# Attention of a two-layer encoder in double steps: scores, values and output splits of two query tiles at a time

## The chip, the cores and the metric

One core of a Trainium2 chip runs the whole kernel. The metric is the device time of one execution in microseconds (us), smaller is better. Engines: TensorE (PE; its weight loads are PEld), VectorE (DVE), ScalarE (ACT), GpSimd (POOL), SyncE (SP, which only issues transfers here).

## The reference

Two layers over x of 512 tokens x 1024 features. Layer 0 mixes tokens by attention, layer 1 by gated linear attention; each is followed by a gated ConvFFN. The change touches the attention alone:

```
def swa_sink_attention(h, w_qkv, sinks, rel_bias, w_o):   # query chunk c (64 tokens) reads key chunks c-1 and c
    qkv = h @ w_qkv                                       # 16 query heads of 64, 4 key/value heads
    ...
    scores = einsum('bnqhgd,bnjhd->bhgnqj', q, k_band) * (A_HEAD_DIM ** -0.5) + bias   # band of 128 keys
    scores = where(valid, scores, NEG)                    # the first chunk has no chunk before it
    m = maximum(scores.max(axis=-1), sink)
    p = exp(scores - m[..., None])
    p = p / (p.sum(axis=-1) + exp(sink - m))[..., None]
    out = einsum('bhgnqj,bnjhd->bnqhgd', p, v_band)
    return out.reshape(B, S, A_HEADS * A_HEAD_DIM) @ w_o
```

## The kernel before

Activations lie feature by token, in 128-row tiles of 512 tokens. Every projection is done in split precision: a weight tile is cast to a rounded high part (ScalarE, `hi_unit`, L950), the low part is raw minus high (VectorE, `lo_unit`, L1389), and TensorE forms high x high, high x low and low x high (`product`, L485). A unit is one 128-column block of outputs: 8 blocks of the contraction, 24 products of 512 columns. Units are numbered: 4 to 11 are the queries (`A_Q` on), 12 to 19 the output projection (`A_O` on). The queries of KV head g need units 4 + 2g and 5 + 2g. A unit u waits for `lo_ready` u + 1 and for its bank; four weight slots are loaded by SyncE as earlier units end.

The attention stage is a hand-written list on each engine, joined by semaphores, with a loop over k = 0 to 15. Step k is KV head g = k // 4 and token tile p = k % 4 (two chunks j, two head halves). TensorE, for k: half a projection unit (or, from k = 12, half of an output unit's contraction), `scores(k)` (L667), `turn_probs(k - 2)` (four transposes, L675), `values(k - 3)` (L685). VectorE, for k: `softmax_max(k)` (adds scale and bias, L1767, row maximum, L1770, and three small ones), at odd k `queries` (L1750), `o_lo(k - 3)` (L1788), `lo_unit`, `softmax_divide(k - 1)` (L1780 to L1782). ScalarE: `probs_copy(k - 2)` (L1206), `o_hi(k - 3)` (L1218), `softmax_exp(k)` (four exponentials with row sums, L1198, and one small), `hi_unit`. In step k = 2 VectorE makes the low part of unit 8, which TensorE starts in step 4, and so on in twos; each engine's list is executed strictly in order.

KT holds the keys of each KV head twice, once with rows 64 to 127 zero and once with rows 0 to 63 zero, so that a contraction over all 128 rows of QT (two heads) picks one head. `values` writes its two head halves to rows 0 to 63 and 64 to 127 of bank B7, from 64 columns of V each. After the loop the output units get the rest of their contraction; the last two blocks of each wait for the last `o_lo`. Before the loop GpSimd fills the bias table (L2028, L2030), and clears KT (L2021, L2022) before SyncE's loads of constants.

Of the kernel before, what the change touches and what calls it, by code (L numbers as in the profile page):

```python
# [31 lines left out]
P = 128  # L32
# [63 lines left out]
def trunk(nc, xT, gains, w_qkv, sinks, rel_bias, w_o, w_bin, w_ga, w_gate, b_norm, w_bo, w_up, conv_w, conv_b,  # L96
          w_down0, w_down1, onehot, ident, causal, causal_pair, out, bias_rows):
    with ExitStack() as ctx:
# [100 lines left out]
        KT = place("KT", [P, KV, 2, T])  # L199
# [6 lines left out]
        BIAS = place("BIAS", [P, KV, 4, P])  # L206
# [265 lines left out]
        def _(pe):  # L472
# [178 lines left out]
            def scores(k):  # L651

                g, p = divmod(k, 4)
                if k == 0:
                    pe.wait_ge(std_ready, 1)
                    pe.wait_ge(v_copied, 4)
                    pe.wait_ge(k_dup, 64)
                if k >= 2:
                    pe.wait_ge(s_ready, k - 1)
                if p == 0:  # L660
                    pe.wait_ge(unit_evac, A_Q + 2 * g + 2)
                for j in range(2):
                    for half in range(2):
                        q, keys = QT[:, g % 2, 2 * p + j], KT[:, g, half]
                        c = (2 * j + half) * P
                        first = max(2 * p - 1 + j, 0) * CHUNK
                        last = mm(PS[:, B4 + k % 2, c:c + P], q, keys[:, first:first + P], start=True, stop=True)  # L667
                last.then_inc(scores_done, 1)
# [9 lines left out]
            def values(k):  # L678
                g, p = divmod(k, 4)
                pe.wait_ge(pt_ready, k + 1)  # L680
                if k >= 1:
                    pe.wait_ge(ol_ready, k)
                for j in range(2):
                    for half in range(2):
                        last = mm(PS[64 * half:64 * half + 64, B7, j * P:(j + 1) * P],  # L685
                                  V[:, 1 - j if p else 0, p, g * HD:(g + 1) * HD], PT[:, k % 2, 2 * j + half],
                                  start=True, stop=True)
# [5 lines left out]
            for k in range(16):  # L693
                g, p = divmod(k, 4)


                if g < 3:
                    u = A_Q + 2 + k // 2
                    if k % 2 == 0:
                        pe.wait_ge(lo_ready, u + 1)  # L700
                        pe.wait_ge(unit_evac, u - 3)
                    last = out_part(u, range(4 * (k % 2), 4 * (k % 2) + 4), XH, XL, k % 2 == 0, k % 2 == 1)
                    if k % 2 == 1:
                        last.then_inc(unit_done, 1)
                else:
                    u = A_O + p
                    pe.wait_ge(lo_ready, u + 1)
                    pe.wait_ge(unit_evac, u - 3)
                    pe.wait_ge(ol_ready, 8)
                    out_part(u, range(0, 4), OH, OL, True, False)  # L710
                scores(k)
                if k >= 2:
                    turn_probs(k - 2)
                if k >= 3:
                    values(k - 3)
            pe.wait_ge(ol_ready, 12)
            out_part(A_O, range(4, 6), OH, OL, False, False)
            turn_probs(14)
            values(13)
            out_part(A_O + 1, range(4, 6), OH, OL, False, False)  # L720
            turn_probs(15)
            values(14)
            out_part(A_O + 2, range(4, 6), OH, OL, False, False)
            values(15)
            out_part(A_O + 3, range(4, 6), OH, OL, False, False)
            pe.wait_ge(ol_ready, 16)
# [218 lines left out]
        def _(act):  # L945
# [227 lines left out]
            for hh in range(2):  # L1173
                for half in range(2):
                    rows = slice(64 * hh, 64 * hh + 64)
                    act.dma_start(BIAS[rows, :, 2 + half],
# [4 lines left out]
            for g in range(KV):  # L1181
# [3 lines left out]
                act.dma_start(KT[there, g, 1 - g % 2], KT[here, g, g % 2]).then_inc(k_dup, 16)  # L1185
# [16 lines left out]
            def probs_copy(k):  # L1202
                act.wait_ge(pt_done, k + 1)
                if k >= 2:
                    act.wait_ge(pv_done, k - 1)
                nc.scalar.copy(PT[:, k % 2], PS[:, B6].rearrange("p (i c) -> p i c", i=4)).then_inc(pt_ready, 1)  # L1206

            def o_view(k):

                return PS[:, B7, 0:2 * P].rearrange("p (j a q) -> p a j q", j=2, a=2)  # L1210

            def o_tiles(t, k):
                g, p = divmod(k, 4)
                return t[:, 2 * g:2 * g + 2, p * P:(p + 1) * P].rearrange("p a (j q) -> p a j q", j=2)

            def o_hi(k):
                act.wait_ge(pv_done, k + 1)
# [960 lines left out]
```

## Time and profile before

| | us |
|---|---|
| median of 3 runs | 1079.18 (1078.86 to 1079.74) |
| the profiled execution, its own time | 1078.77 |
| its span | 1076.9 |
| TensorE busy | 1067.1 (99%) |
| VectorE busy | 752.5 (70%) |
| ScalarE busy | 494.1 (46%) |
| GpSimd busy | 113.8 (11%) |

The profile shows one execution. Busy times are sums over an engine's instructions; the chain that ended last is followed back from the last instruction, at each step to what released it. Matmuls are pipelined: a product's row in the timeline is longer than the distance to the next one's start, and the distance is what it costs. The attention loop lies between about 43 and 128 us.

### The profile page before, as it was taken

Reading aid. Unit: us, or ns where it says so; the run is one execution under the profiler, and the core shown is the slowest. Engines: PE = TensorE matmul, PEld = TensorE weight load, DVE = VectorE, ACT = ScalarE, POOL = GpSimd, SP = SyncE. Lnnn points to the kernel's source line nnn. Section 1 sums busy time; section 2 is a strip of 40 time slices with the busy share of each in tenths; the row PEclk is TensorE's granted clock in tenths of the full one; section 3 lists DMA queues with packets and bytes.
Section 4 is the critical chain, followed back from the end, with each engine's and each line's share of the span. In section 5 each row is a group of like instructions: output and inputs, shape, how many; then the busy total and the mean of one; then the engine's idle time right before and its main releaser. Section 6 shows DMA issues by size and latency. Waiting matters only on the chain.

```text
span 1076.9 us, 15711 instructions
## 1 busy us (share of the span) xinstructions
PE 1067.1 (99%) x5930; PEld 917.5 (85%) x5930; DVE 752.5 (70%) x1097; ACT 494.1 (46%) x769; POOL 113.8 (11%) x108
## 2 busy tenths in 40 slices
PE   9999999999999999999999999999999999999997
PEld 7888788888899888899888888888888899888897
DVE  6588667677876667789644556867676876667786
ACT  7366554434433343455652345454444433334443
POOL 2100030000100000123020321130000100000122
PEclk9999999999999999999999999999999999999999
DMA  7611032226653225552222211222225652225552
GB/s 228 154 59 60 22 115 98 97 97 185 162 134 107 98 97 170 129 140 99 97 74 85 97 40 59 73 105 97 97 97 185 162 147 96 97 97 170 135 141 92
DMA packets 43804, 121.12 MB, mean 112 GB/s; under 512 B 5250, under 2 KB 10530, under 8 KB 43748
## 3 DMA queue, kind: packets, MB, share of 16 engines
q1 hardware_dynamic: 36020, 106.55, 29.7%
q0 software_dynamic: 4608, 11.54, 6.6%
q10 hardware_dynamic: 3120, 2.28, 1.1%
q8 instruction: 37, 0.61, 0.2%
q14 instruction: 19, 0.16, 0.0%
HBM read 116.93 MB, written 2.88 MB: 111 GB/s over the span
## 4 chain that ended last, share of the span: by engine, by line
PE 93%; DVE 4%; DMA 1%; ACT 1%; issue 1%; SPq 0%; POOL 0%; DVEq 0%; POOLq 0%
PE PS L485 69%; PE PS L545 18%; PE PS L667 1%; PE PS L685 1%; DMA DRAW_W<-w_down 1%; PE PS L675 1%; DVE STD L1896 1%; DMA X<-xT 1%; PE PS L836 1%; DVE WL L1389 1%; PE PS L746 0%; PE PS L849 0%; PE PS L773 0%; DVE EU L1900 0%; PE PS L786 0%
## 5 line engine op out<-in xcount | busy, mean ns | idle before, releaser
L485 PE MATMUL PS<-XH,WH 128*128 128x512 f32 x992 | 391.4, 395 | 1.4 <-DVE XL L1406 1.4
L485 PE MATMUL PS<-XH,WL 128*128 128x512 f32 x992 | 386.4, 390 | 0.0
L485 PE MATMUL PS<-XL,WH 128*128 128x512 f32 x992 | 386.1, 389 | 0.0
L485 PEld LDWEIGHTS PS<-XH,WH 128*128 128x128 f32 x992 | 186.2, 188 | 42.5 <-issue 4.6
L485 PEld LDWEIGHTS PS<-XH,WL 128*128 128x128 f32 x992 | 186.2, 188 | 39.1
L485 PEld LDWEIGHTS PS<-XL,WH 128*128 128x128 f32 x992 | 186.3, 188 | 38.8 <-issue 1.0
L950 ACT CAST WH<-WRAW 128x1024 fp32r<-128x1024 f32 x134 | 139.5, 1045 | 158.3 <-DMA WRAW<-w_up 106.9
L1389 DVE TENSOR_TENSOR WL<-WRAW,WH 128x1024 fp32r<-128x1024 f32 x134 | 165.1, 1233 | 16.4 <-ACT WH L950 15.7
L1427 DVE TENSOR_TENSOR GS<-PS,R 128x512 f32<-128x512 f32 x44 | 30.4, 692 | 118.5 <-PE PS L485 118.5
L545 PE MATMUL PS<-AH,DH_Z 128*128 128x256 f32 x352 | 97.7, 278 | 0.2
L545 PE MATMUL PS<-AH,DL_Z 128*128 128x256 f32 x352 | 97.2, 276 | 0.0
L545 PE MATMUL PS<-AL,DH_Z 128*128 128x256 f32 x352 | 97.2, 276 | 0.0
L993 ACT ACTIVATE CV<-GS,CONVB,CONVW 128x512 f32<-128x512 f32 x44 | 36.1, 820 | 91.8 <-DVE GS L1427 91.8
L545 PE MATMUL PS<-AH,DH_W 128*128 128x256 f32 x264 | 73.5, 279 | 0.2
L545 PE MATMUL PS<-AH,DL_W 128*128 128x256 f32 x264 | 72.9, 276 | 0.0
L545 PE MATMUL PS<-AL,DH_W 128*128 128x256 f32 x264 | 72.9, 276 | 0.0
L1522 DVE TENSOR_TENSOR X<-X,PS 128x256 f32<-128x256 f32 x112 | 46.1, 416 | 34.0 <-PE PS L545 33.5
L545 PEld LDWEIGHTS PS<-AH,DH_Z 128*128 128x128 f32 x352 | 66.1, 188 | 2.0 <-PE PS L485 1.9
L545 PEld LDWEIGHTS PS<-AL,DH_Z 128*128 128x128 f32 x352 | 66.1, 188 | 0.0
L545 PEld LDWEIGHTS PS<-AH,DL_Z 128*128 128x128 f32 x352 | 66.1, 188 | 0.0
L1027 ACT CAST DH_W<-DRAW_W 128x768 fp32r<-128x768 f32 (+1 forms) x48 | 37.0, 780 | 53.7 <-DMA DRAW_W<-w_down 53.6
L545 PEld LDWEIGHTS PS<-AH,DH_W 128*128 128x128 f32 x264 | 49.6, 188 | 0.6 <-DVE X L1522 0.6
(236 smaller groups left out, 1508.1 us busy)
## 6 DMA issues: line engine op xcount, KB each, us to landing
WRAW<-w_up SPq DMA_DIRECT2D x88, 512.0 KB, 3.3
WRAW<-w_bin SPq DMA_DIRECT2D x24, 512.0 KB, 3.2
DRAW_W<-w_down SPq DMA_DIRECT2D x24, 384.0 KB, 3.8
DRAW_W<-w_down SPq DMA_DIRECT2D x24, 320.0 KB, 3.0
WSUM_Z<-w_down SPq DMA_DIRECT2D x12, 384.0 KB, 4.7
WSUM_Z<-w_down POOLq DMA_DIRECT2D x12, 384.0 KB, 6.3
WRAW<-w_qkv SPq DMA_DIRECT2D x8, 512.0 KB, 3.4
WSUM_Z<-w_down SPq DMA_DIRECT2D x12, 320.0 KB, 3.8
```

What stands on the lines that cost most here:

```text
L485: last = mm(PS[:, bank], w[:, c:c + P], x[:, kb], start=start and n == 0 and w is wh and x is hi, stop=stop and n == len(kbs) - 1 and w is wl)
L545: last = mm(PS[:, bank, 0:TH], w[:, c], act_part[:, kb, x], start=start and kb == 0 and w is DH[name] and act_part is AH, stop=kb == PAIRS ...
L667: last = mm(PS[:, B4 + k % 2, c:c + P], q, keys[:, first:first + P], start=True, stop=True)
L675: last = nc.tensor.transpose(PS[:, B6, i * P:(i + 1) * P], PB[:, k % 2, i], IDENT[:])
L685: last = mm(PS[64 * half:64 * half + 64, B7, j * P:(j + 1) * P], V[:, 1 - j if p else 0, p, g * HD:(g + 1) * HD], PT[:, k % 2, 2 * j + hal ...
L836: mm(PS[:, B6 + p // 2, (p % 2) * HV:(p % 2 + 1) * HV], KUT[:, p], VV[:, p, h * HV:(h + 1) * HV], start=True, stop=True).then_inc(u_done, 1)
L950: nc.scalar.copy(WH[s][:], WRAW[s][:]).then_inc(hi_ready, 1)
L993: A(CV[:, par], GS[:, par, 2:T + 2], ACT.Identity, bias=CONVB[:, layer, tile], scale=CONVW[:, layer, tile, 2]).then_inc(c0_ready, 1)
L1027: nc.scalar.copy(DH[name][:, c], raw[:, c]).then_inc(down_hi[name], 1)
L1389: tt(WL[s][:], WRAW[s][:], WH[s][:].bitcast(F32), ALU.subtract).then_inc(lo_ready, 1)
L1427: tt(GS[:, par, 2:T + 2], PS[:, 2 * par], R[:], ALU.mult).then_inc(unit_evac, 2)
L1522: tt(x, x, PS[:, SETS[n % 2][bank], 0:TH], op).then_inc(x_taken, 1)
```

## The change

Pairs of token tiles are worked at a time in parts of the lists. `scores(pair)` makes the scores of two tiles at once: KT holds each key head once in both row halves, each product contracts over 64 rows only, head half 0 into bank B4 and half 1 into B5, 16 of TensorE's products per pair in place of 2 x 8. `values(pair)` and the output split (`o_hi`, `o_lo`) also take both tiles at once, 512 columns in place of 256. The transposes stay per tile, each behind one half projection unit (`between(pair, half)`). The softmax stays per tile; its four parts are ordered by head, then chunk. The bias table gets an own copy for the first tile, filled in three GpSimd copies. All four lists are written out anew. VectorE's list of a pair has both `softmax_max` first; `queries` and `lo_unit` stand between the two `softmax_divide`. In pair 1 that is `lo_unit(8)`, and unit 8 is the one of TensorE's pair 2.

```diff
--- before.py
+++ after.py
@@ -196,14 +196,14 @@
         place_at[0] = region
-        KT = place("KT", [P, KV, 2, T])
+        KT = place("KT", [P, KV, T])
         VT = place("VT", [P, 2, T])
...
         PT = place("PT", [P, 2, 4, P])
-        BIAS = place("BIAS", [P, KV, 4, P])
+        BIAS = place("BIAS", [P, 2, KV, 4, P])
         TB = place("TB", [P, REL])
...
@@ -648,23 +648,24 @@
...
-            def scores(k):
-
-                g, p = divmod(k, 4)
+            def scores(pair):
+
+                g, p = pair // 2, 2 * (pair % 2)
+                k = 2 * pair
                 if k == 0:
...
                     pe.wait_ge(k_dup, 64)
-                if k >= 2:
-                    pe.wait_ge(s_ready, k - 1)
+                if k >= 1:
+                    pe.wait_ge(s_ready, k)
                 if p == 0:
                     pe.wait_ge(unit_evac, A_Q + 2 * g + 2)
-                for j in range(2):
+                for j in range(4):
+                    first = max(2 * p - 1 + j, 0) * CHUNK
                     for half in range(2):
-                        q, keys = QT[:, g % 2, 2 * p + j], KT[:, g, half]
-                        c = (2 * j + half) * P
-                        first = max(2 * p - 1 + j, 0) * CHUNK
-                        last = mm(PS[:, B4 + k % 2, c:c + P], q, keys[:, first:first + P], start=True, stop=True)
+                        rows = slice(64 * half, 64 * half + 64)
+                        q, keys = QT[rows, g % 2, 2 * p + j], KT[rows, g]
+                        last = mm(PS[:, B4 + half, j * P:(j + 1) * P], q, keys[:, first:first + P], start=True, stop=True)
                 last.then_inc(scores_done, 1)
             def turn_probs(k):
@@ -675,55 +676,62 @@
...
-            def values(k):
-                g, p = divmod(k, 4)
-                pe.wait_ge(pt_ready, k + 1)
-                if k >= 1:
-                    pe.wait_ge(ol_ready, k)
-                for j in range(2):
-                    for half in range(2):
-                        last = mm(PS[64 * half:64 * half + 64, B7, j * P:(j + 1) * P],
-                                  V[:, 1 - j if p else 0, p, g * HD:(g + 1) * HD], PT[:, k % 2, 2 * j + half],
-                                  start=True, stop=True)
+            def values(pair):
+                g = pair // 2
+                pe.wait_ge(pt_ready, 2 * pair + 2)
+                if pair >= 1:
+                    pe.wait_ge(ol_ready, pair)
+                for k in range(2):
+                    p = 2 * (pair % 2) + k
+                    for j in range(2):
+                        c = (2 * k + j) * P
+                        for half in range(2):
+                            last = mm(PS[64 * half:64 * half + 64, B7, c:c + P],
+                                      V[:, 1 - j if p else 0, p, g * HD:(g + 1) * HD], PT[:, k, 2 * half + j],
+                                      start=True, stop=True)
                 last.then_inc(pv_done, 1)
             def out_part(u, kbs, hi, lo, start, stop):
...
-            for k in range(16):
-                g, p = divmod(k, 4)
-
-
-                if g < 3:
-                    u = A_Q + 2 + k // 2
-                    if k % 2 == 0:
+            def between(pair, half):
+
+                if pair < 6:
+                    u = A_Q + 2 + pair
+                    if half == 0:
                         pe.wait_ge(lo_ready, u + 1)
                         pe.wait_ge(unit_evac, u - 3)
-                    last = out_part(u, range(4 * (k % 2), 4 * (k % 2) + 4), XH, XL, k % 2 == 0, k % 2 == 1)
-                    if k % 2 == 1:
+                    last = out_part(u, range(4 * half, 4 * half + 4), XH, XL, half == 0, half == 1)
+                    if half == 1:
                         last.then_inc(unit_done, 1)
                 else:
-                    u = A_O + p
+                    u = A_O + 2 * (pair - 6) + half
                     pe.wait_ge(lo_ready, u + 1)
                     pe.wait_ge(unit_evac, u - 3)
-                    pe.wait_ge(ol_ready, 8)
+                    pe.wait_ge(ol_ready, 4)
                     out_part(u, range(0, 4), OH, OL, True, False)
-                scores(k)
-                if k >= 2:
-                    turn_probs(k - 2)
-                if k >= 3:
-                    values(k - 3)
-            pe.wait_ge(ol_ready, 12)
+
+            for pair in range(8):
+                between(pair, 0)
+                scores(pair)
+                if pair >= 2:
+                    values(pair - 2)
+                if pair >= 1:
+                    turn_probs(2 * pair - 2)
+                between(pair, 1)
+                if pair >= 1:
+                    turn_probs(2 * pair - 1)
+            pe.wait_ge(ol_ready, 6)
             out_part(A_O, range(4, 6), OH, OL, False, False)
+            values(6)
             turn_probs(14)
-            values(13)
             out_part(A_O + 1, range(4, 6), OH, OL, False, False)
             turn_probs(15)
-            values(14)
-            out_part(A_O + 2, range(4, 6), OH, OL, False, False)
-            values(15)
+            out_part(A_O + 2, range(4, 5), OH, OL, False, False)
+            values(7)
+            out_part(A_O + 2, range(5, 6), OH, OL, False, False)
             out_part(A_O + 3, range(4, 6), OH, OL, False, False)
-            pe.wait_ge(ol_ready, 16)
+            pe.wait_ge(ol_ready, 8)
             for u in range(A_O, A_O + 4):
...
@@ -1173,7 +1181,7 @@
...
                     rows = slice(64 * hh, 64 * hh + 64)
-                    act.dma_start(BIAS[rows, :, 2 + half],
+                    act.dma_start(BIAS[rows, 1, :, 2 * half + 1],
                                   bass.AP(tensor=bias_rows.tensor,
...
@@ -1182,7 +1190,7 @@
...
                 here, there = slice(64 * (g % 2), 64 * (g % 2) + 64), slice(64 - 64 * (g % 2), 128 - 64 * (g % 2))
-                act.dma_start(KT[there, g, 1 - g % 2], KT[here, g, g % 2]).then_inc(k_dup, 16)
+                act.dma_start(KT[there, g], KT[here, g]).then_inc(k_dup, 16)
             hi_unit(6)
...
@@ -1202,38 +1210,30 @@
             def probs_copy(k):
...
                 if k >= 2:
-                    act.wait_ge(pv_done, k - 1)
+                    act.wait_ge(pv_done, k // 2)
                 nc.scalar.copy(PT[:, k % 2], PS[:, B6].rearrange("p (i c) -> p i c", i=4)).then_inc(pt_ready, 1)
-            def o_view(k):
-
-                return PS[:, B7, 0:2 * P].rearrange("p (j a q) -> p a j q", j=2, a=2)
-
-            def o_tiles(t, k):
-                g, p = divmod(k, 4)
-                return t[:, 2 * g:2 * g + 2, p * P:(p + 1) * P].rearrange("p a (j q) -> p a j q", j=2)
-
-            def o_hi(k):
-                act.wait_ge(pv_done, k + 1)
-                nc.scalar.copy(o_tiles(OH, k), o_view(k)).then_inc(oh_ready, 1)
-
-            for k in range(16):
-                g, p = divmod(k, 4)
-                if k >= 2:
-                    probs_copy(k - 2)
-                if k >= 3:
-                    o_hi(k - 3)
-                softmax_exp(k)
-                if k % 2 == 0 and k <= 8:
-                    hi_unit(8 + k // 2)
-                elif 9 <= k <= 12 and k != 10:
-                    hi_unit(k + 3 if k > 9 else 13)
-                elif k == 14:
-                    hi_unit(A_O + 4)
-            for k in range(14, 16):
-                probs_copy(k)
-                o_hi(k - 1)
-            o_hi(15)
+            def o_hi(pair):
+                g, tokens = pair // 2, slice(pair % 2 * TH, pair % 2 * TH + TH)
+                act.wait_ge(pv_done, pair + 1)
+                nc.scalar.copy(OH[:, 2 * g:2 * g + 2, tokens].rearrange("p a (x q) -> p a x q", x=4),
+                               PS[:, B7].rearrange("p (x a q) -> p a x q", x=4, a=2)).then_inc(oh_ready, 1)
+
+            for pair in range(8):
+                if pair >= 2:
+                    o_hi(pair - 2)
+                if pair >= 1:
+                    probs_copy(2 * pair - 2)
+                softmax_exp(2 * pair)
+                for u in ((8,), (9,), (10,), (11,), (12, 13), (14,), (15,), (16,))[pair]:
+                    hi_unit(u)
+                if pair >= 1:
+                    probs_copy(2 * pair - 1)
+                softmax_exp(2 * pair + 1)
+            o_hi(6)
+            probs_copy(14)
+            probs_copy(15)
+            o_hi(7)
             for m in range(6):
...
@@ -1736,7 +1736,7 @@
...
                     rows = slice(64 * half, 64 * half + 64)
-                    last = tt(KT[rows, 2 * t + half, half], PS[rows, t], R[rows], ALU.mult)
+                    last = tt(KT[rows, 2 * t + half], PS[rows, t], R[rows], ALU.mult)
                 last.then_inc(unit_evac, 1)
...
@@ -1758,18 +1758,16 @@
             def softmax_max(k):
...
                 if k == 0:
-                    dve.wait_ge(bias_ready, 2)
-                dve.wait_ge(scores_done, k + 1)
+                    dve.wait_ge(bias_ready, 4)
+                dve.wait_ge(scores_done, k // 2 + 1)
                 b = k % 2
-                items = lambda t: t.rearrange("p (j x) -> p j x", j=2)
-                bias = BIAS[:, g].rearrange("p i c -> p (i c)")
-                bias = items(bias) if p == 0 else bias[:, 2 * P:].unsqueeze(1).to_broadcast([P, 2, 2 * P])
-                stt(items(SB[:, b].rearrange("p i c -> p (i c)")), items(PS[:, B4 + b]), A_SCALE, bias,
+                by_head = lambda t: t.rearrange("p (h j) c -> p h (j c)", h=2)
+                stt(by_head(SB[:, b]), PS[:, B4:B4 + 2, 2 * b * P:2 * (b + 1) * P], A_SCALE, by_head(BIAS[:, min(p, 1), g]),
                     ALU.mult, ALU.add).then_inc(s_ready, 1)
...
                 link(nc.vector.tensor_reduce(MX[:, b], SB[:, b], AX.X, ALU.max))
-                sink = SINK[:, g:g + 1, :].to_broadcast([P, 2, 2])
-                two = lambda t: t[:, b].rearrange("p (j h) -> p j h", j=2)
+                sink = SINK[:, g].unsqueeze(2).to_broadcast([P, 2, 2])
+                two = lambda t: t[:, b].rearrange("p (h j) -> p h j", h=2)
                 link(tt(two(MX), two(MX), sink, ALU.max))
...
@@ -1781,32 +1779,27 @@
...
-            def o_lo(k):
-                g, p = divmod(k, 4)
-                dve.wait_ge(oh_ready, k + 1)
-                view = lambda t: t[:, 2 * g:2 * g + 2, p * P:(p + 1) * P].rearrange("p a (j q) -> p a j q", j=2)
-                tt(view(OL), PS[:, B7, 0:2 * P].rearrange("p (j a q) -> p a j q", j=2, a=2), view(OH).bitcast(F32),
+            def o_lo(pair):
+                g, tokens = pair // 2, slice(pair % 2 * TH, pair % 2 * TH + TH)
+                dve.wait_ge(oh_ready, pair + 1)
+                view = lambda t: t[:, 2 * g:2 * g + 2, tokens].rearrange("p a (x q) -> p a x q", x=4)
+                tt(view(OL), PS[:, B7].rearrange("p (x a q) -> p a x q", x=4, a=2), view(OH).bitcast(F32),
                    ALU.subtract).then_inc(ol_ready, 1)
-            for k in range(16):
-                g, p = divmod(k, 4)
-                softmax_max(k)
-
-                if g < 3 and k % 2 == 1:
-                    queries(A_Q + 2 + k // 2)
-                if k >= 3:
-                    o_lo(k - 3)
-                if k % 2 == 0 and 2 <= k <= 10:
-                    lo_unit(7 + k // 2)
-                elif 11 <= k <= 13:
-                    lo_unit(k + 2)
-                if k >= 1:
-                    softmax_divide(k - 1)
-            softmax_divide(15)
-            o_lo(13)
+            for pair in range(8):
+                softmax_max(2 * pair)
+                softmax_max(2 * pair + 1)
+                if pair >= 2:
+                    o_lo(pair - 2)
+                softmax_divide(2 * pair)
+                if pair < 6:
+                    queries(A_Q + 2 + pair)
+                for u in ((), (8,), (9,), (10,), (11,), (12, 13), (14, 15), ())[pair]:
+                    lo_unit(u)
+                softmax_divide(2 * pair + 1)
+            o_lo(6)
             lo_unit(A_O + 4)
-            o_lo(14)
-            o_lo(15)
+            o_lo(7)
             for m in range(6):
...
@@ -2017,18 +2010,19 @@
...
             pool.wait_ge(eps_set, 1)
-            link(nc.gpsimd.memset(WG[:], 0.0))
-            link(nc.gpsimd.memset(KT[64:P, :, 0], 0.0))
-            nc.gpsimd.memset(KT[0:64, :, 1], 0.0).then_inc(small_set, 1)
+            nc.gpsimd.memset(WG[:], 0.0).then_inc(small_set, 1)
             pool.wait_ge(small_set, 1)
...
             pool.wait_ge(bias_in, 16 * 4)
-            nc.gpsimd.memset(BIAS[:, :, 0:2, 64:P], NEG).then_inc(bias_ready, 1)
+            nc.gpsimd.memset(BIAS[:, 0, :, ::2, 64:P], NEG).then_inc(bias_ready, 1)
             pool.wait_ge(bias_ready, 1)
-            nc.gpsimd.tensor_copy(BIAS[:, :, 0:2, 0:64], BIAS[:, :, 2:4, 64:P]).then_inc(bias_ready, 1)
-            pool.wait_ge(bias_ready, 2)
+            loaded = BIAS[:, 1, :, 1::2]
+            for n, (to, src) in enumerate(((BIAS[:, 0, :, ::2, 0:64], BIAS[:, 1, :, 1::2, 64:P]),
+                                           (BIAS[:, 0, :, 1::2], loaded), (BIAS[:, 1, :, ::2], loaded))):
+                nc.gpsimd.tensor_copy(to, src).then_inc(bias_ready, 1)
+                pool.wait_ge(bias_ready, n + 2)
...
             pool.wait_ge(consts, 16 * CONSTS)

```

## Rows read from the trace of the kernel before

**Rows 1.** Page, part 4: the chain that ended last, its shares by engine.

```profile
PE 93%; DVE 4%; DMA 1%; ACT 1%; issue 1%; SPq 0%; POOL 0%; DVEq 0%; POOLq 0%
```

**Rows 2.** Windows: busy us (and instructions) of PE, PEld, DVE, ACT, POOL; granted clock.

```profile
46.00:128.40 82.40, 81.52 (x527) 66.69 (x526) 62.90 (x159) 51.74 (x185) 0.00 (x0) 1.00 0.14 47
```

**Rows 3.** Chain in order of time (start us, us, what) for one step.

```profile
74.47 2.94 PE PS L485 x12
77.42 0.89 PE PS L667 x8
...
79.33 2.94 PE PS L485 x12
```

**Rows 4.** Timeline of TensorE (start us, us, line, output, inputs), one step and the end.

```profile
83.00 0.60 PE L675 MATMUL PS<-IDENT,PB 128*128 128x128 f32 x4
...
83.53 0.33 PE L685 MATMUL PS<-PT,V 128*64 128x128 f32 x2
...
83.53 0.55 PE L685 MATMUL PS<-PT,V 128*64 128x128 f32 x6
...
84.46 0.39 PE L485 MATMUL PS<-XL,WH 128*128 128x512 f32 x1
...
128.36 0.40 PE L485 MATMUL PS<-OH,WH 128*128 128x512 f32 x1
```

**Rows 5.** Timeline of VectorE over one step of the loop.

```profile
80.14 0.69 DVE L1750 TENSOR_TENSOR QT<-PS,R 128x512 f32<-128x512 f32 x1
80.74 0.42 DVE L1788 TENSOR_TENSOR OL<-PS,OH 128x256 fp32r<-128x256 f32 x1
...
83.20 0.69 DVE L1767 SCALAR_TENSOR_TENSOR SB<-PS,BIAS 128x512 f32<-128x512 f32 x1 [1.04 <-PE PS L667]
...
85.00 0.41 DVE L1788 TENSOR_TENSOR OL<-PS,OH 128x256 fp32r<-128x256 f32 x1
85.33 1.21 DVE L1389 TENSOR_TENSOR WL<-WRAW,WH 128x1024 fp32r<-128x1024 f32 x1
86.47 0.15 DVE L1780 TENSOR_TENSOR RD<-SUM,ES 128x4 f32<-128x4 f32 x1
...
86.86 0.69 DVE L1782 TENSOR_TENSOR PB<-PB,RD 128x512 f32<-128x512 f32 x1
```

**Rows 6.** Timeline of ScalarE over one step of the loop.

```profile
78.78 0.59 ACT L1206 COPY PT<-PS 128x512 f32<-128x512 f32 x1 [0.70 <-PE PS L675]
79.38 0.37 ACT L1218 CAST OH<-PS 128x256 fp32r<-128x256 f32 x1
80.27 0.40 ACT L1198 ACTIVATE PB<-SB,NM 128x128 f32<-128x128 f32 x1 [0.52 <-DVE NM L1775]
...
81.83 0.19 ACT L1200 ACTIVATE ES<-SM 128x4 f32<-128x4 f32 x1
```

**Rows 7.** Timeline of the other queues before the loop, and its first scores.

```profile
5.20 1.92 SPq L413 DMA_DIRECT2D WRAW<-w_qkv  x3
...
39.94 0.61 POOL L2030 COPY BIAS<-BIAS 128x512 f32<-128x512 f32 x1
...
46.18 1.05 PE L667 MATMUL PS<-KT,QT 128*128 128x128 f32 x8
...
47.35 0.69 DVE L1767 SCALAR_TENSOR_TENSOR SB<-PS,BIAS 128x512 f32<-128x512 f32 x1 [3.00 <-PE PS L667]
```

**Rows 8.** Windows (last columns: granted clock, DMA share, GB/s) and timeline of TensorE, first and last products.

```profile
1.00 2.93 PE L622 MATMUL PS<-STD 128*128 128x128 f32 x12 [1.00 <-POOL STD L2016]
...
3.72 1.47 PE L622 MATMUL PS<-STD 128*128 128x128 f32 x11
...
1070.80 0.72 PE L922 MATMUL PS<-STD,ONESR 128*128 128x128 f32 x5
...
1075.70:1076.80 1.10, 0.00 (x0) 0.50 0.28 90
```

**Rows 9.** Waits of TensorE in this stretch: us in total, times, longest.

```profile
PE PS L675 <- DVE PB L1782: 0.9, 2, 0.7
```

## The prediction

> **What bounds the kernel now.** I read the page first: TensorE holds 93% of the chain that ended last [rows 1]. So a change pays only if it takes work off TensorE without making TensorE wait. Next the stage table for the attention stretch, 46 to 128.4 us: TensorE 81.5 of 82.4 us, VectorE 62.9, ScalarE 51.7 [rows 2]. VectorE has a quarter of the stretch free and ScalarE more than a third, but only because each has work of neighbouring steps to interleave. Then the chain: it never leaves TensorE over most of the loop, and one step from a half projection unit (2.94) over scores (0.89), transposes and values to the next half unit is 79.33 - 74.47 = 4.86, so two steps take 9.72 [rows 3]. The stretch ends at 128.36, where the last two blocks of the output units begin [rows 4]. Last the timelines of the three engines over one step [rows 4 to 6]. Times below are from the span's start. A duration that is followed by more work counts from start to start.
>
> **TensorE's part.** A plain product of 512 columns takes 0.228 (the 2.94 of 12, less 0.21 that belongs to the values before them, below), so a half unit takes 2.74. Scores: 8 products (each f32 product is two in the trace) of 0.11 make 0.89. Transposes: 4 x 0.11 = 0.44. Values already work in two column halves: two products start together and each further two add 0.11 ((0.55 - 0.33)/2), so 8 take 0.44 [rows 4]. Their step is dearer than that. The transposes began at 83.00 and were through at 83.44, and the next unit's second product starts at 84.46, which without any cost of changing shape would be 83.44 + 0.44 + 0.23 = 84.11. So one burst in halves costs 0.35 on top: 0.14 going in (0.09 before the first pair, 0.05 in it), 0.21 coming out. I cost a values burst at 0.80 now.
> After the change scores run as two 64-row halves into two banks, for which the trace has no row. The nearest are those values: 16 products in 8 pairs, 0.88 + 0.35 = 1.22 where two bursts of 0.89 took 1.78. From below, with no cost of changing, it is 0.88; from above, with no overlap, 1.78 + 0.35 = 2.12. I take 1.22, since both are halves of the array used in turn. Values of a pair: 0.87 + 0.35 = 1.22 for 1.60. The work per pair on TensorE falls from 9.72 to 2 x 2.74 + 1.22 + 1.22 + 2 x 0.44 = 8.8. Over 8 pairs that is 4.5 + 3.0 = 7.5 us less.
> The Trainium skill (TensorEngine Tiling (Array Packing), Key Properties) says that switching the tiling mode drains the engine, and the same page (Theoretical Speedup) gives up to 2x for a contraction of 64. The 0.35 above agrees with the drain. By the 2x alone scores would take 0.88 and the total below would be 2.1 us less; by the drain it stands as I have it.
>
> **Where the weights' low parts go.** This decides it. Before, `lo_unit(8)` runs in step 2 and its unit starts in step 4, `lo_unit(9)` in step 4 for step 6: two steps of slack. After, VectorE's list puts `lo_unit(8)` into pair 1, behind both `softmax_max`, `softmax_divide(2)` and `queries`, and TensorE's pair 2 *begins* with unit 8 and waits for it; the same with 9, 10, 11, 12 and 14 in pairs 2 to 6. Behind that wait stand the half unit and the next scores, on which VectorE's next pair waits. So the two engines take turns, and the loop is their sum.
> VectorE's leg, from the end of the last score product: start 0.20 later (83.20 against 83.00); two `softmax_max` of 1.80 (83.20 to 85.00), 3.60; `o_lo` of a pair, 512 columns from PSUM, 0.60 (as the QT row, 80.14 to 80.74); divide 0.40 + 0.60 = 1.00; queries 0.60; low part 1.21; and 0.15 until TensorE has its first product through [rows 4, 5]. Sum 7.36.
> TensorE's leg: half unit 2.74, scores to the end of their last product 0.14 + 0.88 = 1.02. The loop is 11.1 us.
> ScalarE has a side leg into it: scores' coming out 0.21, values 1.22 and 0.14, `o_hi` of 512 columns 0.60 and the copy of the transposes 0.60 (78.78 to 79.38), four exponentials and the small one 1.75 (80.27 to 82.02) [rows 6]: the divide can start at 4.55, where VectorE comes to it at 4.40. If scores and values, which stand side by side, share one change of shape, these 0.15 go. I take half: **11.2 us per pair, against 9.72**. TensorE works 8.8 of them and stands idle 2.4.
> The wait of the units for `unit_evac` and of scores for `s_ready` are met long before: nothing.
>
> **The sum.** Scores of pair 0 start at 46.18 [rows 7]. 1.22 and two half units: scores of pair 1 at 52.9, done 53.9. VectorE: 47.4 + 3.6 = 51.0, divide(0) behind its exponentials to 52.1, the second ones (behind ScalarE's cast of unit 8) end at 53.8, divide(1) at 54.9; then 3.6, 0.1 of waiting, divide, queries and low part give 61.4. TensorE was through at 57.8, idles 3.8, and starts scores of pair 2 at 64.3. Four more turns of 11.2: 109.0. The last has no queries, 10.6: scores of pair 7 at 119.6. Behind them TensorE has, without a wait over 0.1: 1.22 + 1.22 + 0.44 + 2.74 + 0.44, then 6 products 1.37, values 1.22, 0.44, 1.37, 0.44, 0.68, values 1.3, 0.68, 1.37 = 14.9: 134.5. Before it was 128.36 [rows 4]. The difference is **+6.2 us**.
> Against the profiled execution that is 1076.9 + 6.2 = 1083.1 of span and 1078.8 + 6.2 = 1085.0 of time; that run lay 0.4 below the median of the three, so the median should be 1079.2 + 6.2 = **1085.4**. After the stretch TensorE's queue is the same and it is the bound, so nothing gives the loss back.
>
> **Edits that cost nothing.** The bias table is completed by two more GpSimd copies of 1024 columns; one of 512 took 0.61, so they add 2.5 at most, and the table is ready at 43.1 where the first use is at 47.35: cover 4.2, and every us beyond it would be lost whole [rows 7]. The constants for GA behind them (0.96 and less each) are used some 350 us later. Two memsets of KT go from GpSimd; SyncE, which waits for them before it issues the constants, is itself busy issuing weights until 7.1 [rows 7], so that earlier memsets start nothing earlier. The copies of K between halves move the same bytes on the same queue. The mask and the sink only change order.
>
> **The rivals.** *No overlap of row halves.* 0.9 more in each of six turns, in pair 0 to 1 and in little else: 6.6 more, 1092.0. For it: no row shows 64-row halves. Against: column halves overlap fully [rows 4].
> *The clock falls in the gaps.* At the end the granted clock is 0.50, that is 1.2 GHz, from 1075.7, and the last product had ended at 1071.4: 4.3 us without work [rows 8]. At the start products come every 0.23 ((2.93 - 0.4)/11) from 1.0 until 3.7, and from 3.72 every 0.11 ((1.47 - 0.35)/10): 2.7 us at the low level, so a fall costs some 1.4. The first gap is 3.8, the others 2.4, all shorter than 4.3. One fall gives 1086.8, six 1093.6. The Trainium skill (TensorE: Matmul & The Clock Gate, on throughput drops) warns that idle gaps between bursts send the engine back to half rate; the rows agree that idle time does it, and have no gap of 2.4 or 3.8.
> *TensorE stays the bound.* If the low part is ready when TensorE comes to it, the kernel gains the 7.5 and the 0.9 of waits for PB [rows 9]: 1070.8, faster. It needs a turn of 8.8, VectorE's 7.36 down to 5.0; the gain ends where the turn is 10.2. Against: all its terms are measured on the same shapes, and the order is in the queues. A turn between 10 and 10.4 is the case of no difference.
>
> **How the numbers follow.** Forecast 0.80; no overlap 0.07; clock 0.04; TensorE bound 0.05; in between, no difference 0.04. So slower 0.91, same 0.04, faster 0.05, with 0.2% as about what a measurement of this kernel tells from no change. The forecast's own range is 1082 (scores at 0.88, shapes changed for nothing) to 1088. The range takes in the upper bound of the row halves, 1092.5, and leaves out the gain.
>
> **What would show it.** The chain should run through WL, QT, PB and SB in the stretch; TensorE should wait some 3.8 + 4 x 2.4 + 1.8 = 15 us for WL, six times; the first output block should start near 134.5; two score products should start within 0.01 of each other. I am wrong if TensorE does not wait for WL, or if scores of successive pairs stand 8.8 or over 12 us apart.

## The result and the profile after

The changed kernel takes 1091.1 us (median of 5, 1089.66 to 1091.48) against 1079.56 for the one before (median of 5): ratio 1.0107, 95% interval 1.0096 to 1.0118. Slower by 11.5 us, where 6.2 were forecast. The profiled execution took 1089.66, with a span of 1087.9: 11.0 more than the span before. The median lies 1.4 above it. That is about the price of one more fall of the clock (below), but that execution left no trace, so this is a guess.

The page of the changed kernel: TensorE's busy tenths and the clock it was granted, each in 40 slices of 27 us, and the shares of the chain.

```profile
PE   9978899999999999999999999999999999999997
...
PEclk9989999999999999999999999999999999999999
...
PE 89%; DVE 7%; ACT 2%; DMA 1%; issue 1%; SPq 0%; POOL 0%; DVEq 0%; POOLq 0%
```

TensorE holds 89% of the chain where it held 93% [rows 1]. VectorE's share is 7% for 4%, ScalarE's 2% for 1%, and in the third to fifth slices of TensorE's row (54 to 136 us, the attention) it is no longer busy all the time; the clock's third slice shows a dip that was not there before. The timeline of TensorE, of the lines that matter: every start of a pair's scores (L668), and every product that had to wait (in brackets: how long, and for whom). L485 is a product of a unit, WL the low part of its weights.

```profile
53.21 1.16 PE L668 MATMUL PS<-KT,QT 64*128 64x128 f32 x16
...
61.61 0.74 PE L485 MATMUL PS<-XH,WH 128*128 128x512 f32 x1 [3.47 <-DVE WL L1389]
...
66.16 1.16 PE L668 MATMUL PS<-KT,QT 64*128 64x128 f32 x16
...
74.43 0.50 PE L485 MATMUL PS<-XH,WH 128*128 128x512 f32 x1 [2.28 <-DVE WL L1389]
...
78.96 1.16 PE L668 MATMUL PS<-KT,QT 64*128 64x128 f32 x16
...
87.23 0.50 PE L485 MATMUL PS<-XH,WH 128*128 128x512 f32 x1 [2.28 <-DVE WL L1389]
...
90.20 1.16 PE L668 MATMUL PS<-KT,QT 64*128 64x128 f32 x16
...
98.47 0.50 PE L485 MATMUL PS<-XH,WH 128*128 128x512 f32 x1 [2.29 <-DVE WL L1389]
...
103.00 1.16 PE L668 MATMUL PS<-KT,QT 64*128 64x128 f32 x16
...
111.27 0.50 PE L485 MATMUL PS<-OH,WH 128*128 128x512 f32 x1 [2.29 <-DVE WL L1389]
...
114.21 1.16 PE L668 MATMUL PS<-KT,QT 64*128 64x128 f32 x16
...
121.89 0.50 PE L485 MATMUL PS<-OH,WH 128*128 128x512 f32 x1 [1.70 <-DVE WL L1389]
```

Six waits for WL, of 3.5, four times 2.3, and 1.7 us, 14.3 together, where the kernel before had 0.9 for PB [rows 9] and the forecast some 15. The scores of pairs 1 to 7 start 12.95, 12.80, 11.24, 12.80, 11.21 and 10.6 us apart (a turn; the last pair's start at 124.83), where two steps took 9.72 [rows 3]. The forecast had 11.4, 11.2 and 10.6. So three turns are as worked out, and three are 1.55 to 1.6 too long. What sets a turn is in the chain, here of the fourth, from the scores to the next unit's products:

```profile
90.27 1.12 PE PS L668 x16
...
95.99 0.69 DVE PB L1780
96.69 0.60 DVE QT L1750
97.28 1.14 DVE WL L1389
...
98.47 4.60 PE PS L485 x12
```

The chain goes over to VectorE behind the scores and comes back only with WL, 7.1 us later: the engines take turns. Why that turn is 12.80 and not 11.2 is in the windows (columns: busy PE, PEld, DVE, ACT, POOL; granted clock, DMA share, GB/s).

```profile
61.70:65.10 3.40, 3.40 (x8) 2.67 (x9) 1.03 (x3) 0.05 (x1) 0.00 (x0) 0.50 0.00 0
65.10:74.40 9.30, 7.04 (x57) 5.46 (x55) 6.73 (x16) 5.97 (x22) 0.00 (x0) 1.00 0.17 55
75.40:78.80 3.40, 3.40 (x9) 2.34 (x8) 0.14 (x1) 0.00 (x0) 0.00 (x0) 0.50 0.00 0
99.30:102.60 3.30, 3.30 (x9) 2.61 (x8) 1.02 (x3) 0.00 (x0) 0.00 (x0) 0.50 0.00 0
```

In three stretches of about 3.4 us (one row for each that shows the half clock) TensorE was granted half the clock (1.2 GHz), each beginning within 1 us after one of the gaps, in the half unit that everybody waits for. After the other gaps of 2.3 us it was not. A turn with such a stretch is 12.80, one without 11.24.

One mark serves all comparisons below, the product of L506, the first work behind the output units: everything that the attention loses or gains is in by then. From the chain of the kernel before, and of the changed one:

```profile
161.18 0.23 PE PS L506
```

```profile
172.32 0.23 PE PS L506
```

11.1 us lost by there, and 11.0 over the span. Nothing is given back or lost later.

What TensorE itself takes. Timeline of one pair of the changed kernel, scores, values, and the transposes after them:

```profile
90.20 1.16 PE L668 MATMUL PS<-KT,QT 64*128 64x128 f32 x16
91.29 1.09 PE L689 MATMUL PS<-PT,V 128*64 128x128 f32 x16
92.32 0.66 PE L676 MATMUL PS<-IDENT,PB 128*128 128x128 f32 x4
```

Scores take 1.09 and values 1.03, 2.12 together for 32 products that stream in 16 pairs of 0.11, 1.76. Before, a pair of steps took 2 x 0.89 and 2 x 0.80 for them. The halves of 64 rows do overlap. The 2.12 leaves out what the change of shape costs before the first and behind the last of these products. Counted as the prediction counted its 0.35, from the product before to the second product behind, the two bursts cost 0.50 over their streaming (a burst: all scores, or all values, of a step or pair).

### The profile page after: what moved, and what is told of

Read it like the earlier page. It is cut to its first block, busy times and chain, and to the rows that moved or that the text cites. A ratio compares the mean times of both kernels' runs of the same rounds, so it can differ in the third digit from the quotient of the medians.

```text
span 1087.9 us, 15687 instructions
## 1 busy us (share of the span) xinstructions
PE 1065.7 (98%) x5930; PEld 914.5 (84%) x5930; DVE 751.3 (69%) x1089; ACT 491.3 (45%) x761; POOL 113.4 (10%) x108
## 4 chain that ended last, share of the span: by engine, by line
PE 89%; DVE 7%; ACT 2%; DMA 1%; issue 1%; SPq 0%; POOL 0%; DVEq 0%; POOLq 0%
PE PS L485 65%; PE PS L545 19%; DVE WL L1389 1%; DVE MX L1768 1%; DVE SB L1765 1%; PE PS L668 1%; DMA X<-xT 1%; DVE STD L1889 1%; PE PS L844 1%; DVE PB L1780 0%; DVE SS L1710 0%; ACT PB L1206 0%; PE PS L754 0%; DMA DRAW_W<-w_down 0%; PE PS L857 0%
## 5 line engine op out<-in xcount | busy, mean ns | idle before, releaser
L485 PE MATMUL PS<-XH,WH 128*128 128x512 f32 x992 | 393.4, 397 | 10.3 <-DVE WL L1389 10.3
L485 PE MATMUL PS<-XL,WH 128*128 128x512 f32 x992 | 388.1, 391 | 0.0
L485 PE MATMUL PS<-XH,WL 128*128 128x512 f32 x992 | 388.1, 391 | 0.0
L485 PEld LDWEIGHTS PS<-XH,WH 128*128 128x128 f32 x992 | 187.1, 189 | 51.1 <-DVE WL L1389 11.3
L485 PEld LDWEIGHTS PS<-XH,WL 128*128 128x128 f32 x992 | 187.5, 189 | 39.8
L485 PEld LDWEIGHTS PS<-XL,WH 128*128 128x128 f32 x992 | 187.5, 189 | 39.2 <-issue 1.0
L545 PE MATMUL PS<-AH,DH_Z 128*128 128x256 f32 x352 | 97.7, 278 | 0.2
L545 PE MATMUL PS<-AH,DL_Z 128*128 128x256 f32 x352 | 97.3, 276 | 0.0
L545 PE MATMUL PS<-AL,DH_Z 128*128 128x256 f32 x352 | 97.3, 276 | 0.0
L545 PE MATMUL PS<-AH,DH_W 128*128 128x256 f32 x264 | 73.5, 279 | 0.1
L545 PE MATMUL PS<-AH,DL_W 128*128 128x256 f32 x264 | 73.0, 276 | 0.0
L545 PE MATMUL PS<-AL,DH_W 128*128 128x256 f32 x264 | 73.0, 276 | 0.0
L545 PEld LDWEIGHTS PS<-AH,DH_Z 128*128 128x128 f32 x352 | 66.1, 188 | 1.9 <-PE PS L485 1.9
L545 PEld LDWEIGHTS PS<-AL,DH_Z 128*128 128x128 f32 x352 | 66.2, 188 | 0.0
L545 PEld LDWEIGHTS PS<-AH,DL_Z 128*128 128x128 f32 x352 | 66.1, 188 | 0.0
L545 PEld LDWEIGHTS PS<-AH,DH_W 128*128 128x128 f32 x264 | 49.6, 188 | 0.3 <-DVE X L1522 0.3
```

The lines of the kernel that those rows point to most:

```text
L485: last = mm(PS[:, bank], w[:, c:c + P], x[:, kb], start=start and n == 0 and w is wh and x is hi, stop=stop and n == len(kbs) - 1 and w is wl)
L545: last = mm(PS[:, bank, 0:TH], w[:, c], act_part[:, kb, x], start=start and kb == 0 and w is DH[name] and act_part is AH, stop=kb == PAIRS ...
```

## The experiments

Theory A is that of the prediction, with the clock added: the low parts of the weights are made in the pair before their use, behind everything else of VectorE, so that TensorE and VectorE take turns; and the gaps that this opens make the clock fall. Theory B, in e1, is that the double step itself is the loss; the others are in each expectation. Each median is set against the runs of the kernel before on the same chip: 1079.57 for the first four, 1078.90 for the last three.

**e1, low parts one pair earlier.**

```diff
-                for u in ((), (8,), (9,), (10,), (11,), (12, 13), (14, 15), ())[pair]:
+                for u in ((8,), (9,), (10,), (11,), (12, 13), (14,), (15,), ())[pair]:
                     lo_unit(u)
```

> The changed kernel with VectorE's low parts one pair earlier (units 8, 9, 10, 11, 12 and 13, 14, 15 in pairs 0 to 6 in place of 1 to 6), all else the same. Theory A (TensorE and VectorE take turns because the low part is made in the pair before its use, behind everything else, and the clock falls in the gaps that this opens): the waits of TensorE for WL go, scores of successive pairs stand 8.7 us apart, no fall of the clock in the stretch; 1071, between 1069 and 1073. Theory B (the double step itself costs: long bursts, two shapes of the array, both softmax_max in a row): the waits move to another place, and the time stays over 1079.

Measured 1070.24 (1069.63 to 1071.26), ratio 0.9917, interval 0.9900 to 0.9935. TensorE's timeline:

```profile
60.66 1.16 PE L668 MATMUL PS<-KT,QT 64*128 64x128 f32 x16
...
69.31 1.16 PE L668 MATMUL PS<-KT,QT 64*128 64x128 f32 x16
```

Its window (busy PE; clock, DMA share, GB/s), and the mark:

```profile
44.00:120.00 76.00, 75.95 (x540) 1.00 0.17 57
```

```profile
151.75 0.23 PE PS L506
```

Pairs are 8.65 us apart (one of them, from pair 5 to 6, 8.95), no product of TensorE waits in the stretch, and the granted clock is 1.00 over it. The mark lies 9.4 before that of the kernel before, 20.6 before that of the changed kernel. The place of the low parts in VectorE's list is the whole loss and 9 us more. Theory B falls. This is the fastest of all versions here.

**e2, the gaps filled.** The products go into the bank that the unit is about to start, and are overwritten.

```diff
                     if half == 0:
-                        pe.wait_ge(lo_ready, u + 1)
                         pe.wait_ge(unit_evac, u - 3)
+                        for _ in range({2: 14, 3: 9, 4: 9, 5: 9}.get(pair, 0)):
+                            mm(PS[:, u % 4, 0:P], ONES, ONES, start=True, stop=True)
+                        pe.wait_ge(lo_ready, u + 1)
```

and the same for pairs 6 and 7 (9 and 6 products) in the other branch.

> The changed kernel with TensorE kept at work while it waits for the low part: 14 f32 products of 128 columns into the still empty bank before unit 8, 9 each before units 9 to 12, 6 before unit 14, each 0.22 us at full clock. Nothing else changes. Theory A: the clock is 1.00 over the whole stretch, all turns are 11.2 us (the last 10.6), and what the falls cost goes: 1.6 each for three or four falls, 1086 (1085 to 1087). Theory B (the falls have another cause than the gaps, say the products of half the array's rows): the clock falls as before and the time stays at 1091. Theory C (the filling delays the real work by more than it saves): over 1091.

Measured 1087.00 (1086.25 to 1088.26), ratio 1.0069, interval 1.0050 to 1.0087.

```profile
70.22 2.17 PE L704 MATMUL PS<-ONESR 128*128 128x128 f32 x18
72.69 0.50 PE L485 MATMUL PS<-XH,WH 128*128 128x512 f32 x1 [0.29 <-DVE WL L1393]
...
75.67 1.16 PE L668 MATMUL PS<-KT,QT 64*128 64x128 f32 x16
...
86.89 1.16 PE L668 MATMUL PS<-KT,QT 64*128 64x128 f32 x16
```

```profile
44.00:136.00 92.00, 90.16 (x653) 74.26 (x652) 62.44 (x152) 48.72 (x177) 1.77 (x5) 1.00 0.14 47
```

```profile
167.46 0.23 PE PS L506
```

The waits shrink to 0.3 (the two longest are 0.35). The turns are 11.35, then 11.2 to 11.3, the last 10.6, though the low part comes no earlier: the filling (L704) took only time that was idle. The granted clock is 1.00. The mark is 6.3 later than before, against 11.1 in the changed kernel: the three falls had cost 4.9, and what is left is the forecast's +6.2. The time came out at the upper end of what theory A allowed; 3.3 us of the profiled run's loss arose behind the mark (its span is 1086.5, 9.6 over that of before, and its time 1088.26 the slowest of the four), in work that the edit doesn't touch. 0.9 of it is one wait of TensorE (L545, for VectorE's DL_Z) that the traces of before, the changed kernel and e1 do not have; the cause of the rest is open. In the other eight profiles the stretch behind the mark varies by 1.7 us from run to run, so the mark compares the attention more sharply than the medians do.

**e4, the low part ahead of divide and queries.**

```diff
+                for u in ((), (8,), (9,), (10,), (11,), (12, 13), (14, 15), ())[pair]:
+                    lo_unit(u)
                 softmax_divide(2 * pair)
                 if pair < 6:
                     queries(A_Q + 2 + pair)
-                for u in ((), (8,), (9,), (10,), (11,), (12, 13), (14, 15), ())[pair]:
-                    lo_unit(u)
                 softmax_divide(2 * pair + 1)
```

> The changed kernel with lo_unit ahead of the first divide and of queries in VectorE's list of a pair, still in the pair before its use. Theory A: VectorE's leg is shorter by the divide and the queries, 1.6 us, so turns are 9.6 apart, TensorE's gaps are about 0.9, the clock doesn't fall: 9.4 and the 4.9 of the falls less than 1091.1, 1077 (1075.5 to 1078.5). Theory B (something else than this leg sets the turn, such as ScalarE's exponentials): turns stay at 11.2 and the time over 1085.

Measured 1076.52 (1075.53 to 1077.64), ratio 0.9971, interval 0.9961 to 0.9980.

```profile
62.41 1.16 PE L668 MATMUL PS<-KT,QT 64*128 64x128 f32 x16
...
69.07 0.50 PE L485 MATMUL PS<-XH,WH 128*128 128x512 f32 x1 [0.68 <-DVE WL L1389]
...
72.04 1.16 PE L668 MATMUL PS<-KT,QT 64*128 64x128 f32 x16
```

```profile
157.99 0.23 PE PS L506
```

The dose answers as it should: 1.6 us off VectorE's leg take 1.6 off the turn (9.6 each), five waits are 0.7 and the first is 1.74, and the clock holds behind all of them. The mark is 3.2 earlier than before. The kernel is faster than before already here, with the low parts still made in the pair before their use.

**e5, half rows alone, in single steps.** The new layouts of KT and BIAS and the new scores go into the kernel before; the lists stay. Scores of a step write both banks, so they wait for the bias addition of the step before:

```diff
-                if k >= 2:
-                    pe.wait_ge(s_ready, k - 1)
+                if k >= 1:
+                    pe.wait_ge(s_ready, k)
...
-                        q, keys = QT[:, g % 2, 2 * p + j], KT[:, g, half]
-                        c = (2 * j + half) * P
+                        q, keys = QT[rows, g % 2, 2 * p + j], KT[rows, g]
+                        c = (2 * (k % 2) + j) * P
                         first = max(2 * p - 1 + j, 0) * CHUNK
-                        last = mm(PS[:, B4 + k % 2, c:c + P], q, ...
+                        last = mm(PS[:, B4 + half, c:c + P], q, ...
```

> The kernel before with one part of the change alone: scores in two halves of 64 rows into banks B4 and B5 (one bank for each half, so that scores of a step wait for the bias addition of the step before), with the new layout of keys and bias, but still one token tile per step and the old lists. Theory A (a burst in halves costs 0.35 on top of half the streaming time): a scores burst takes 0.44 + 0.30 to 0.35 in place of 0.89, 16 times 0.1 to 0.15, 1077.2 (1076.5 to 1078.2). Theory B (halving the rows is the gain and changing shape is nearly free): 16 times 0.4, 1073. Theory C (the added wait for the bias addition stalls TensorE): over 1080.

Measured 1078.27 (1077.71 to 1080.04), ratio 0.9993, interval 0.9983 to 1.0002: no difference that can be told, and just above the range of theory A. Theory C falls: TensorE waits for PB alone, 0.8 in all.

```profile
81.82 0.71 PE L668 MATMUL PS<-KT,QT 64*128 64x128 f32 x8
...
86.60 0.71 PE L668 MATMUL PS<-KT,QT 64*128 64x128 f32 x8
```

A step is 4.78 where it was 4.86 [rows 3]: 0.08 for halving the streaming of the scores, 0.44. The change of shape, 0.35 for a burst in halves, eats nearly all of it, now twice in each step. Two steps stream for 9.02 without any change of shape, and for 8.12 with half rows. What is left for the changes is 0.70 in the kernel before (9.72 - 9.02), 1.44 in e5 (9.56 - 8.12) and 0.53 in e1 (8.65 - 8.12). So the half rows gain little alone, 0.08 a step, and (9.72 - 8.65) / 2 = 0.53 a step in e1, where the double step puts scores and values side by side. Double steps without the half rows were not run.

**e3, half the filling.** As e2, with 7, 4 and 3 products in place of 14, 9 and 6.

> The changed kernel with half the filling of e2: 7 products before unit 8, 4 each before units 9 to 12, 3 before unit 14. TensorE is left without work for 1.9 us before unit 8, 1.4 before the next four, 1.1 before unit 14, where it was 3.5, 2.3 and 1.7. Theory A1 (a fall needs a long gap): no fall, the product of L506 starts 6.3 after that of the kernel before, 1086 to 1087. Theory A2 (idle time adds up, so shorter gaps still cause falls, only fewer): one or two falls, 1087.5 to 1089.5. Theory B (filling doesn't matter): three or four falls, 1091.

Measured 1087.08 (1085.19 to 1088.25), ratio 1.0070, interval 1.0053 to 1.0087. TensorE's timeline behind the first two gaps, the window of the clock, and the mark:

```profile
61.52 0.50 PE L485 MATMUL PS<-XH,WH 128*128 128x512 f32 x1 [1.92 <-DVE WL L1393]
...
74.34 0.50 PE L485 MATMUL PS<-XH,WH 128*128 128x512 f32 x1 [1.41 <-DVE WL L1393]
```

```profile
62.60:65.90 3.30, 3.30 (x9) 2.33 (x7) 0.20 (x1) 0.00 (x0) 0.00 (x0) 0.50 0.00 0
```

```profile
169.13 0.23 PE PS L506
```

One fall, behind the first gap, though TensorE was left without work for only 1.92 us at a stretch and had worked 1.7 us before it; none behind the four gaps of 1.4 and the last of 1.0. The mark is 8.0 later than before: 6.3 and one fall of 1.6. The median lies between the ranges of A1 (to 1087) and A2 (from 1087.5) and decides nothing; the trace does, with one fall for A2's one or two. It shows that an idle spell of 1.9 us can be enough. Whether shorter spells before it add up, as A2 has it, no run shows.

**e6, one gap.** As e1, but `lo_unit(8)` stays in pair 1: `((), (8, 9), (10,), (11,), (12, 13), (14,), (15,), ())`.

> The changed kernel with low parts one pair earlier as in e1, but for unit 8, which stays late (8 and 9 both in pair 1). One wait of TensorE for WL is left, 3.5 us before unit 8. Theory A with a fall at this gap: scores of pair 2 start 12.9 after those of pair 1, all later pairs 8.7 apart, 1070.2 + 3.8 + 1.6 = 1075.6. Theory A without a fall: 11.3 apart, 1074.0. Theory B (one late pair is caught up later): 1071.

Measured 1075.07 (1074.90 to 1075.72), ratio 0.9964, interval 0.9950 to 0.9978.

```profile
52.71 1.16 PE L668 MATMUL PS<-KT,QT 64*128 64x128 f32 x16
...
61.12 0.50 PE L485 MATMUL PS<-XH,WH 128*128 128x512 f32 x1 [3.48 <-DVE WL L1389]
...
65.66 1.16 PE L668 MATMUL PS<-KT,QT 64*128 64x128 f32 x16
...
74.32 1.16 PE L668 MATMUL PS<-KT,QT 64*128 64x128 f32 x16
```

One wait of 3.48, one turn of 12.95, then 8.66. A single late weight part costs 4.8 us against e1 by the medians, 5.5 when each is set against its own runs of the kernel before, and 5.3 by the turns: 3.8 for coming late (11.4, as in the forecast and in e2, for a turn of 7.6 in e1) and 1.55 for the fall (12.95 - 11.4). The time lies between theory A with a fall (1075.6) and without (1074.0); the turn of 12.95 tells that there was one. Nothing of it is caught up later, because TensorE has no slack behind.

**e7, the changed kernel once more.**

> The changed kernel as it is, for another look at which gaps end in a fall of the clock. Theory A: turns are either 11.2 (no fall) or 12.8 us (fall), the first 11.4 or 13.0, and nothing between by much; 1089.5 to 1092. The falls may be at other gaps than in the first look.

Measured 1090.21 (1089.31 to 1090.38), ratio 1.0100, interval 1.0083 to 1.0117.

```profile
65.09 1.44 PE L668 MATMUL PS<-KT,QT 64*128 64x128 f32 x16
...
76.61 1.16 PE L668 MATMUL PS<-KT,QT 64*128 64x128 f32 x16
...
84.88 0.50 PE L485 MATMUL PS<-XH,WH 128*128 128x512 f32 x1 [2.29 <-DVE WL L1389]
...
89.22 1.32 PE L668 MATMUL PS<-KT,QT 64*128 64x128 f32 x16
```

```profile
86.30:89.40 3.10, 3.10 (x10) 1.99 (x10) 0.00 (x0) 0.00 (x0) 0.00 (x0) 0.50 0.00 0
110.30:113.40 3.10, 3.10 (x10) 1.97 (x8) 0.67 (x1) 0.00 (x0) 0.00 (x0) 0.50 0.00 0
```

Again three falls (the windows are of the second and third), now behind the first, third and fifth gap (the first profile had the first, second and fourth): 65.09 to 76.61 is 11.5, part of whose length is the end of the first fall, 76.61 to 89.22 is 12.6. A fall may begin in the half unit and reach into the scores (here they take 1.44 and 1.32 instead of 1.16), so turns between 11.2 and 12.8 occur, which the expectation had ruled out. Which of the gaps of 2.3 us brings a fall is not fixed from run to run; that the first gap does was so in all four profiles that have it at 1.9 or 3.5 us, and not in e4, where it is 1.74.

## Why the prediction was right, and what it mis-sized

**The bound and the turn-taking were right.** The step on the weights' low parts named the queue order, the wait and the loop. The turn was worked out at 11.2, and 11.24 and 11.21 were measured where the clock held; the turn without queries at 10.6, and it was 10.6; the first wait at 3.8, it was 3.5; the others at 2.4, they were 2.3. e2 isolates the sum: 6.3 at the mark for a forecast of 6.2. e4 and e1 show that it is VectorE's leg with the low part in it, and no other.

**The rival that should have been in the sum was the clock.** The direction, slower, was right, but the central value missed 5 of 11 us. That the range held the time was luck: the forecast's own range ended at 1088, and 1091.1 fell inside only because the bound of 1092.5 had been taken in for row halves that do not overlap, which they do. One of the prediction's own signs of being wrong also came: three turns were over 12 us. The step that failed is the sentence "all shorter than 4.3". It took the one idle stretch that the trace showed before a fall [rows 8] as the length that a fall needs. That row gives only a length at which the clock had fallen; from below it bounds nothing, since the longest other wait of TensorE in the trace before is 1.1 us, and I gave the rival 0.04. In the runs it fell after all three gaps of 3.5 us, after four of the eight of 2.3 in the changed kernel's two profiles, and after the one of 1.9 in e3. The count of falls, three, lay between the one and the six that I had priced. The price of one was put at 1.4, by the pace of products at the start of the kernel, though the profile's granted clock reads 1.00 there; by the turns it is 1.55 to 1.6. The Trainium skill (TensorE: Matmul & The Clock Gate, Why this matters for your kernels, in the row on throughput drops) advises against idle gaps between bursts of products. The traces agree for the gaps of 3.5 us, with a fall behind each of three. The page's row is on gaps longer than 2.3 us, so the falls behind gaps of 2.3 and 1.9 go beyond it, and its warning alone would not have given three.

**TensorE's own savings were a little under-sized.** I had 2 x 0.35 for the two changes of shape of a pair, at most 0.15 less; side by side they cost 0.50, and TensorE's work of a pair is 8.65 where I had 8.8. The turn-taking of the changed kernel hid this. In e1, where TensorE is the bound, it shows: the rival "TensorE stays the bound" had 8.4 of gain, and 9.4 is there at the mark; seven turns at 0.15 less are about the difference. The tail behind the last scores was put at 14.9 and takes 14.7.

**The rival of no overlap fell**: 16 products in 1.09 to 1.16. The price of a change of shape held for a burst that stands alone: in e5, with two of them in each step, half the streaming saved 0.08 a step.

**The edits costed at nothing cost nothing.** The three GpSimd copies took 3.9 where I had allowed 3.1 with the old one, and hid all the same:

```profile
40.57 3.86 POOL L2024 COPY BIAS<-BIAS 128x512 f32<-128x512 f32 x3
```

They end at 44.4, and the first use is at 47.7, just behind its scores: 3.3 us of cover are left.

## What to carry to other kernels

When two engines pass work back and forth in hand-written lists, look for each wait at how many steps ahead its producer stands, not only at the sums of work: the changed kernel was busy for less time on every engine (TensorE 1065.7 us for 1067.1, VectorE 751.3 for 752.5) and lost 1%, since one producer moved from two steps ahead to directly ahead of its consumer. Put work that depends on nothing in the loop (here the low parts of weights) one round earlier than needed. And when a change opens gaps on TensorE, price the clock with them: a gap costs itself, and behind three of three gaps of 3.5 us and four of eight of 2.3 it cost another 1.6 us here.

## What the runs showed that I had not expected

- The granted clock fell to half within 1.5 us behind gaps of 3.5 and 2.3 us, and of 1.9 us in e3, and stayed there for 3.4 us. It did not behind three gaps of 1.7 us (two in the changed kernel's profiles, one in e4), nor behind those of 1.4, 1.0, 0.7 or 0.3 us, nor behind four of eight of 2.3, and which of these it was changed between the two profiles. What decides it is open.
- Work of no use in the gaps, 0.22 us a product, made the kernel about 4 us faster though it brought nothing forward (7.4 over the kernel before on the same chip, against 11.5 and 11.3 without it).
- Two bursts in halves of different kinds, rows and then columns, side by side, cost 0.50 us over their streaming together, where one burst alone cost 0.35.
